# Score products of the low query part on half of the TensorE array, two PSUM banks side by side

## The reference, cut to what matters

```python
q = rms_norm(q.reshape(B, S, H, 2, Dh), q_g)          # H = 8, Dh = 64
k = rms_norm(k.reshape(B, S, H, 2, Dh), k_g)
s = jnp.einsum('bqhmd,bshmd->bhmqs', qi, k) * scale    # the scores of one block of 128 queries
s = jnp.where(mask, s, -jnp.inf)                       # chunks of 64 keys, causal
p = jax.nn.softmax(s, axis=-1)
pd = p[:, :, 0] - lam * p[:, :, 1]
o = jnp.einsum('bhqs,bshe->bqhe', pd, v)
```

## Time and profile before

| | us |
|---|---|
| median of 3 runs (lowest, highest) | 2846.42 (2845.59, 2848.49) |
| the profiled execution, its own time | 2845.15 |
| its span in the trace | 2843.4 |
| TensorE busy with matmuls | 2736.3 (96%) |
| TensorE busy with weight loads, beside the matmuls | 2374.4 (84%) |
| VectorE busy | 1899.5 (67%) |
| ScalarE busy | 1504.2 (53%) |
| GpSimd busy | 1081.3 (38%) |
| L559, 640 matmuls | 254.3 |
| L561, 640 matmuls | 232.6 |

### The profile page before, as it was taken

How to read it: one execution, slowest core, us unless ns; L and a number is a source line. 1 busy time by engine, 2 the same in 40 slices (tenths; PEclk the granted TensorE clock), 3 DMA queues, 4 the chain that set the end, 5 groups by cost and what they waited for, 6 DMA issues and landing times. The chain is left out here.

```text
span 2843.4 us, 42848 instructions
## 1 busy us (share of the span) xinstructions
PE 2736.3 (96%) x14784; PEld 2374.4 (84%) x14784; DVE 1899.5 (67%) x2726; ACT 1504.2 (53%) x2987; POOL 1081.3 (38%) x956
## 2 busy tenths in 40 slices
PE   7999999999999999979899899999999999999999
PEld 7898989889898989867777678888888888888887
DVE  6777787777777777765676566555555556666655
ACT  5666666666666666664454334444444444444443
POOL 5633334243333425241001254444444444444443
PEclk9999999999999999989999999999999999999999
DMA  7742424243242424224444986666666876666663
GB/s 261 263 138 88 156 95 161 88 144 111 97 147 95 152 92 142 81 94 147 155 163 158 354 301 239 264 265 245 257 266 266 324 287 237 234 240 239 238 239 133
DMA packets 181808, 544.09 MB, mean 191 GB/s; under 512 B 14736, under 2 KB 88208, under 8 KB 136592
## 3 DMA queue, kind: packets, MB, share of 16 engines
q1 hardware_dynamic: 180608, 541.91, 52.2%
q10 hardware_dynamic: 1040, 0.13, 0.0%
HBM read 470.81 MB, written 71.17 MB: 191 GB/s over the span
## 5 line engine op out<-in xcount | busy, mean ns | idle before, releaser
L2102 PE MATMUL banks<-u,w 128*128 128x512 f32 x2688 | 614.3, 390 | 5.1 <-issue 5.1
L417 PE MATMUL banks<-w_hi,u_ring 128*128 128x384 f32 x2048 | 589.6, 348 | 11.9 <-DVE w_lo L396 4.8
L2102 PEld LDWEIGHTS banks<-u,w 128*128 128x128 f32 x2688 | 505.8, 188 | 110.6 <-issue 5.5
L2126 PE MATMUL banks<-w,a_hi 128*128 128x512 f32 x1792 | 553.1, 390 | 5.2 <-POOL w L1877 4.2
L1877 POOL TENSOR_TENSOR w<-w_raw,w 128x1024 fp32r<-128x1024 f32 x96 | 247.1, 2587 | 544.7 <-ACT w L1922 274.2
L601 ACT ACTIVATE p_all<-banks,bias 128x1024 f32<-128x1024 f32 (+7 forms) x384 | 330.8, 864 | 135.7 <-DVE bias L581 67.7
L2126 PEld LDWEIGHTS banks<-w,a_hi 128*128 128x128 f32 x1792 | 337.0, 188 | 76.1 <-POOL w L1877 4.6
L417 PEld LDWEIGHTS banks<-w_hi,u_ring 128*128 128x128 f32 x2048 | 376.2, 189 | 16.7 <-issue 10.7
L2126 PE MATMUL banks<-w,a_lo 128*128 128x512 f32 x896 | 349.3, 390 | 0.0
L447 POOL TENSOR_TENSOR qk_rs<-qk_var,minus_half 128x4 f32<-128x4 f32 x128 | 129.4, 1011 | 573.6 <-DVE qk_var L441 573.6
L417 PE MATMUL banks<-w_lo,u_ring 128*128 128x384 f32 x1024 | 344.8, 337 | 0.0
(11 more groups left out here) (149 smaller groups left out, 4743.7 us busy)
## 6 DMA issues: line engine op xcount, KB each, us to landing
u<-u_factors SPq DMA_DIRECT2D x224, 1024.0 KB, 8.7
u_ring<-u_scratch SPq DMA_DIRECT2D x112, 1024.0 KB, 5.2
w_raw<-in_mlp_w SPq DMA_DIRECT2D x128, 512.0 KB, 6.5
u_scratch<-u_ring SPq DMA_DIRECT2D x16, 1024.0 KB, 5.0
w_raw<-in_a_w_in SPq DMA_DIRECT2D x96, 128.0 KB, 4.9
u_factors<-q_hi SPq DMA_DIRECT2D x23, 512.0 KB, 3.6
u_factors<-q_lo SPq DMA_DIRECT2D x23, 512.0 KB, 3.7
p_all<-in_x SPq DMA_DIRECT2D x16, 512.0 KB, 5.7
```

The source lines that it names most:

```text
L417: last = pe.matmul(proj[:, 0:3 * HD], u[:, part, kt, :], w[:, kt, :], start=(kt == 0 and part == 0 and w is w_hi), stop=(kt == KT - 1 and ...
L2102: last = pe.matmul(banks[:, UP_BANKS[p] + f, :], w[:, 2 * k2 + k, f * P:(f + 1) * P], u[:, :, part, k, :], start=(STARTS[p] and k2 == 0 an ...
L2126: last = pe.matmul(banks[:, DOWN_BANKS[p] + t, :], a[:, p % 2, f, t * P:(t + 1) * P], b[:, f, :], start=(STARTS[p] and f == 0 and a is a_h ...
```

## The change

1. `k_s` no longer has the key's low part always in the upper partitions. `high_half(m, bank)` gives the partitions of the high part: the lower ones where map plus bank is even, the upper ones where it is odd. VectorE writes the low part over the other half, now in two instructions of 64 partitions by 128 keys, one to a map, in place of one of 64 partitions by 256.
2. The product of `q_lo` takes 64 rows of the array alone, those where the key's high part lies, so that the low parts of both are no longer multiplied. Two banks next to each other use different halves of the array. Where a piece is a single bank in a step of three banks, the product stays on all 128 rows.
3. The order in a piece: first the `q_hi` products of its banks, then the `q_lo` products. Steps of one bank (t = 0 to 3) do the `q_hi` products of both maps first, then the `q_lo` products of both maps, which also lie in different halves.
4. Waits on `k_lo_set` count two to a tile.

```diff
-            pe.wait_ge(k_lo_set, last[1] + 1)
+            pe.wait_ge(k_lo_set, 2 * (last[1] + 1))
...
+    def high_half(m, bank):
+        return slice(DH, P) if (m + bank) % 2 else slice(0, DH)
...
-        dve.tensor_tensor(k[low, :, rows], turned(slot, 1, low), k[low, :, rows].bitcast(F32), ALU.subtract)\
-           .then_inc(k_lo_set, 1)
+        for m in range(2):
+            low = high_half(m, j // TPB + 1)
+            dve.tensor_tensor(k[low, m, rows], turned(slot, 1, low)[:, m, :], k[low, m, rows].bitcast(F32),
+                              ALU.subtract).then_inc(k_lo_set, 1)
...
+    def pe_high_scores(pe, a, m, k):
+        h, t = split(a)
+        rows = slice(t * P, (t + 1) * P)
+        first, banks, place = pieces_of(t, m)[k]
+        if LAST_USERS[a, m, k]:
+            pe.wait_ge(exp_done, max(piece_count(*user) for user in LAST_USERS[a, m, k]))
+        for bank in range(first, first + banks):
+            at, width = place + bank - first, bank_width(t, bank)
+            masked = bank == banks_of(t) - 1 and not own_mask(t)
+            if masked:
+                pe.matmul(scores[:, at, width - DH:width], mask_l[:, :], mask_r[:, :],
+                          start=True, stop=False, skip_group_check=True)
+            pe.matmul(scores[:, at, 0:width], q_hi[:, m, rows], k_s[h % 2][:, m, bank * BANK:bank * BANK + width],
+                      start=not masked, stop=False, skip_group_check=True)
+
+    def pe_low_scores(pe, a, m, k):
+        h, t = split(a)
+        rows = slice(t * P, (t + 1) * P)
+        first, banks, place = pieces_of(t, m)[k]
+        for bank in range(first, first + banks):
+            at, width = place + bank - first, bank_width(t, bank)
+            part = slice(0, P) if banks == 1 and banks_of(t) > 1 else high_half(m, bank)
+            last = pe.matmul(scores[:, at, 0:width], q_lo[part, m, rows],
+                             k_s[h % 2][part, m, bank * BANK:bank * BANK + width],
+                             start=False, stop=True, skip_group_check=True)
+        last.then_inc(scored, 1)
...
-            pe.wait_ge(k_lo_set, a + 1)
+            pe.wait_ge(k_lo_set, 2 * (a + 1))
             pe.wait_ge(q_lo_set, a + 1)
...
+        if banks_of(t) == 1:
+            pe_high_scores(pe, a, m, 0)
+            if m == 1:
+                pe_low_scores(pe, a, 0, 0)
+                pe_low_scores(pe, a, 1, 0)
+            return
+        for k in range(count_of(t)):
+            pe_high_scores(pe, a, m, k)
+            pe_low_scores(pe, a, m, k)
```

More of the change, by code:

```diff
@@ L529, in dve_turned_qk @@
         hp, j = split(n)
-        slot, rows, low = slot_of("qk", n), slice(j * P, (j + 1) * P), slice(DH, P)
+        slot, rows = slot_of("qk", n), slice(j * P, (j + 1) * P)
         k = k_s[hp % 2]
```

## The result

| | before | after |
|---|---|---|
| median, us (lowest, highest) | 2846.01 (2844.37, 2848.49) | 2874.85 (2872.77, 2875.19) |
| the profiled execution, us | 2845.15 | 2875.09 |

The changed kernel takes 28.8 us more. The ratio is 1.0099, with a 95% interval of 1.0082 to 1.0117. No change was forecast; the result is slower, inside the range, and close to the 2872 us of the first rival.

The account below looks back on a forecast made before the run. TensorE was taken to bound steps t = 2 to 7 and VectorE t = 8 to 15; seven heads at -1.7 + 1.5 = -0.2 us gave -1.4, so a 2845 us median, no change. Range 2834 to 2905.

Parts of the forecast that it names:

- the first rival: TensorE's array drains at each change of rows while loads run ahead: 0.33 us a group, 2872 us; chance 0.18.
- the long steps: Steps t = 8 to 15, all taken to go at VectorE's pace: TensorE's saving shortens none, VectorE adds 1.5 us a head.
- the 20.4 us of waits on `pt_lo`: TensorE's longest wait in attention, 33 times, the starting point for finding which steps VectorE paces.
- I take 0: Cost on TensorE of going from 128 rows to 64 and back: taken as 0, bounds 0 and 0.27 us.
- the short steps: Steps t = 2 to 7, taken to go at TensorE's pace: all of TensorE's saving there shortens them, 1.70 us a head.
- the two drain rivals: Array drains at each change of rows, loads running ahead (2872 us, chance 0.18) or held back too (2942 us, 0.22).
- The saving by pairing: On TensorE two half-array products run side by side, costing the wider one: 6.7 us a head, 53 us in all.
- the second rival: TensorE's array drains and loads are held back too: 0.65 us a group, 2942 us or about 2890; chance 0.22.
- VectorE's second instruction: One subtraction of 0.428 us becomes two of 0.292 with a 0.03 gap: 0.19 us extra in each step t = 8 to 15.
- no score product stands in it: Loop through VectorE in t = 15, 737.25 to 751.22: TensorE's part is only the values and one set of transposes.
- Order and waits at nothing: The new order of score products and the changed counts of waits on `k_lo_set` were taken to cost nothing.
- The last head at nothing: In the last head TensorE is busy 233 of 268 us and waits for others: no gain taken, bounds 0 and 6.7.

Follow-up runs that it names:

- no_low_long: The kernel before without the `q_lo` products in steps of t = 8 and more, that part of the scores missing: 2846.2 us, 1.0001.
- same_half: Kernel before with the change's product order and every pair's two low products on the lower 64 rows, so they cannot run side by side: 2905.2 us, 1.0206.
- full_rows: The changed kernel with every low product on all 128 rows, keeping layout, order and the two VectorE subtractions: 2848.4 us, 1.0008.
- no_low_short: The kernel before without the `q_lo` products in steps of t below 8, that part of the scores missing: 2829.2 us, 0.9942.
- dve_split: The kernel before with the subtraction for the key's low part split in two, both in the upper partitions: 2850.5 us, 1.0016.
- order_only: The kernel before with only the change's order of products, all on 128 rows, and VectorE's single subtraction: 2845.5 us, 0.9999.
- burst: The changed kernel with two-bank steps (t = 4 to 7) doing four high products, then four half products as two pairs: 2858.5 us, 1.0041.
- bank_burst: Changed kernel with the key's high half chosen by bank alone, one subtraction, half products only in t = 4 to 7, behind the four high products: 2840.0 us, 0.9971.
- low_lower: The kernel before with the key's low part written in the lower partitions and the high part left in the upper ones: 2832.3 us, 0.9948.
- split_lower: The kernel before with the key's low part in the lower partitions, written by two subtractions in place of one: 2834.4 us, 0.9959.
- pairs_long: The changed kernel with half products only in steps of t = 8 and more, other low products on 128 rows: 2857.0 us, 1.0035.
- each_half: The kernel before with every `q_lo` product on the lower 64 rows, nothing paired, two changes of rows to each: 3026.0 us, 1.0623.

## Why the prediction was wrong

**What bounds the kernel: right.** Steps 2 to 7 go at TensorE's pace and the long steps, in the main, at VectorE's. no_low_long took 12 us a head off TensorE in the long steps and gained nothing. Only t = 9 was put down wrongly: it got 0.57 us shorter. And the 20.4 us of waits on `pt_lo` that the prediction began with say less of the long steps than it took them to: 11.1 of them are four waits in the last head.

**The step that failed: "I take 0" for a change between 128 and 64 rows.** The prediction took 0 for this cost; it measured 0.19 us, between the bounds of 0 and 0.27. That made the short steps longer and put TensorE back into the loop of the long ones. I had taken the row of a matmul followed by transposes as the nearest one. Those are changes of type and width on the same 128 rows, and say nothing of a change of rows. The rule that spoke against it stood in the text: the Trainium skill's "TensorEngine Tiling (Array Packing)", Key Properties, has a change of mode drain TensorE. The trace agrees: the load waits until the matmul in front is nearly through (0.07 us before the end of its record). Where a rule names the very thing that the change adds and no row bears on it, its case should be the likeliest. By the chances it was: the two drain rivals had 0.40 together and the forecast 0.38, and the stated time followed the smaller one.

**The saving by pairing: right.** 3 to 4 ns between starts, one width's time for two, 34 us between same_half and the changed kernel (less VectorE's part), where 53 was TensorE's whole saving and the long steps can show only part of it.

**The rivals.** The first, "the array drains, loads run ahead", gave 2872 us at 0.33 a group. The kernel took 2874.9 at 0.38 a group. Its size was nearly right and its picture was not: it let loads run ahead, and they don't; they wait as in the second rival. That it came within 3 us is in part luck. It gave the seven heads 26.6 us where they took 24.5, and the other 5.4 of the 29.9 come from places where it had nothing. The second, at 0.65 a group, was too dear, since it put a load between the two halves, and their loads run together, and since it had the whole 0.16 of the pipeline to empty where about 0.1 is seen.

**Short steps: the sign failed with the price.** Forecast 1.7 us a head shorter; measured 1.9 longer against full_rows (t = 2 to 7: 0.17, 0.14, 0.45, 0.47, 0.38, 0.30). With the 1.7 that the pairing saves, the 10 groups cost 3.6: 0.36 each on the mean, 0.38 in t = 6 and 7. And had the change been free there, "all of it" would still have been too much: in no_low_short a third was returned at t = 8, where TensorE waits 0.84 us for ScalarE's exponential.

**Long steps: TensorE did enter the loop.** I had no price on TensorE there. The steps t = 12 to 14 are 0.22, 0.48 and 0.28 longer than before, of which VectorE's second instruction is 0.04 to 0.07 by full_rows. For the rest, TensorE has run out of slack: its idle time in t = 13, 14 and 15 was 0.14, 0.27 and 0.41 us before, and after it is at most 0.02 in each of t = 12 to 15. Step t = 15 after, columns as in the earlier trace rows:

```profile
754.33:768.61 14.28, 14.26 (x93) 11.40 (x91) 11.64 (x20) 10.50 (x24) 6.81 (x7) 1.00 0.24 79
```

In t = 13 the lateness also shows as a wait of VectorE (after):

```profile
732.08 1.95 DVE L653 SCALAR_TENSOR_TENSOR p_all<-p_all,neg_c 128x1664 f32<-128x1664 f32 x1
734.24 1.23 DVE L608 TENSOR_REDUCE mx<-banks 128x1 f32<-128x1024 f32 x1 [0.20 <-PE banks L573]
```

and what it waits for:

```profile
733.05 0.71 PE L563 MATMUL banks<-k_s,q_hi 128*128 128x512 f32 x2
733.69 0.50 PE L573 MATMUL banks<-k_s,q_lo 64*128 64x512 f32 x2
```

VectorE is free at 734.03, and the pair ends at 734.19. In t = 10 and 11, where each map has one pair, TensorE still idles for 0.29 us and the steps are those of full_rows. The sentence "no score product stands in it" held only while the scores of map 1 were early enough.

**VectorE's second instruction: mis-sized.** Forecast 0.19 us a long step, measured 0.03 to 0.09 for each in dve_split. I had put a gap of 0.03 between the two and counted both in full, because the rows around L536 showed that gap. It belongs to the change of partitions, of which there are two with one subtraction or with two. The split turned one instruction of 0.43 us into two of 0.29 that overlap by 0.08 in dve_split: 0.07 more.

**Order and waits at nothing: right** (order_only, 0.9999). **The last head at nothing:** its attention steps are 0.5 us longer together, and 0.9 more come behind them. From the start of the last head to the end order_only, whose products are all whole, differs from the kernel before by 0.3 us and full_rows by 1.5, so 1.4 is no more than such scatter.

**The sum, mended.** Short steps +1.9, long steps +1.2 from TensorE, VectorE +0.4: 3.5 a head, 24.5 in seven heads. The 1.0 up to the end of the first head, the two slow first steps (3.2) and the last head (1.4), less the 0.2 of the third head, bring it to the 29.9 of the profiled spans.

**Open.** In the two long first steps the granted clock falls (after, columns as in the earlier trace rows; the stretch before, and the stretch itself):

```profile
938.00:943.00 5.00, 3.69 (x28) 3.26 (x27) 3.40 (x8) 2.18 (x8) 5.00 (x4) 1.00 0.49 197
943.00:947.30 4.30, 4.25 (x21) 4.01 (x20) 0.83 (x2) 0.60 (x1) 1.66 (x3) 0.60 0.02 4
```

TensorE was at 2.4 GHz, idle for 1.3 of the 5 us before, and then for most of 4.3 us at 1.2 GHz. The profiled executions of full_rows, dve_split, same_half, burst, no_low_long, bank_burst, low_lower and split_lower have one such step each, those of before, order_only, pairs_long and no_low_short none; each_half has two in other places (t = 15 of the first head and t = 12 of the fourth). One profiled execution of each does not show whether the change makes it more frequent; it is 3 of the 29 us.

## What to carry to other kernels

Half-array products side by side have to stand in bursts: a change of rows costs 0.19 us on each side, so one pair of 512 columns (0.23 saved) loses and two pairs about break even. Longer bursts weren't tried. Before counting what a change saves on an engine, ask in which steps that engine sets the pace, and how much slack the others have left, for an engine that is late enough enters a loop it was not in. On VectorE keep instructions that follow each other on the same first partition: moving a 64-partition operand from the upper to the lower half was worth 0.5% of this kernel.

## What the runs showed of the hardware that was not expected

- A load that changes the number of rows is held until about 0.07 us before the end of the record in front (662.93 against 662.50 + 0.50). At 2.4 GHz this was 0.071 to 0.073 us ahead of every pair of the changed kernel, behind matmuls of 128, 256, 384 and 512 columns alike, and 0.066 to 0.073 behind pairs of two times 512. Two loads of the two halves start 3 to 4 ns apart, as their matmuls do.
- VectorE: a start at another partition costs 0.11 us on each side, two sides to a subtraction. Over seven heads, 1.7 us each, that was 12 of the 14.6 us that low_lower gained.
- The record of the same subtraction is 0.40 us in the lower half, where it overlaps its neighbours, and 0.43 in the upper half, where it doesn't.
